# Eight experts of a mixture layer: the 128-column weight block as the stationary operand, loaded as two halves of 64 columns, with 96 token slots moving

## What is computed

```python
D_MODEL = 1024; SEQ = 256; N_EXPERTS = 8; TOP_K = 2; D_FF_EXPERT = 3584

def swiglu(h, w13, w2):
    gate, up = jnp.split(h @ w13, 2, axis=-1)
    return (jax.nn.silu(gate) * up) @ w2

def moe_swiglu(h, router, w13, w2):
    t = h.reshape(B * S, D)
    logits = (t @ router).astype(jnp.float32)
    top_val, top_idx = lax.top_k(logits, TOP_K)
    gate = jax.nn.softmax(top_val, axis=-1)
    combine = jnp.einsum('tk,tke->te', gate, jax.nn.one_hot(top_idx, N_EXPERTS, dtype=jnp.float32))
    out = jnp.zeros_like(t)
    for e in range(N_EXPERTS):
        out = out + combine[:, e:e + 1].astype(t.dtype) * swiglu(t, w13[e], w2[e])
```

## Time and profile before

| | |
|---|---|
| median of three runs | 2245.45 us (2242.42 to 2260.5) |
| the profiled execution's own time | 2243.6 us |
| its span, first to last instruction | 2241.8 us |
| granted TensorE clock, mean over the span | 0.983 |
| TensorE busy | 2155.9 us |
| VectorE (DVE) busy | 760.2 us |
| ScalarE (ACT) busy | 265.0 us |
| read from HBM | 460.96 MB |

### The profile page before, as it was taken

One profiled execution on the slowest core, in us unless ns is written; L12 is line 12 of the kernel. 1 busy time (PEld: TensorE's weight loads), 2 busy tenths in 40 slices (PEclk: granted clock), 3 DMA queues, 4 the chain that ended last, 5 costly groups with the idle time before them and its releaser, 6 DMA issues.

```text
span 2241.8 us, 20009 instructions
## 1 busy us (share of the span) xinstructions
PE 2155.9 (96%) x7476; PEld 1191.3 (53%) x7476; DVE 760.2 (34%) x2080; ACT 265.0 (12%) x549; POOL 192.6 (9%) x318
## 2 busy tenths in 40 slices
PE   8999989999799999997999999999999999999998
PEld 4454456776455788984444444444444444444443
DVE  2131231000343556533333343333423434324322
ACT  2121130000012333521000000000000000000000
POOL 1111101000103344220000000000000000000000
PEclk9999999999899899998999999999999999999999
DMA  9433425445410110027799999999899999999991
GB/s 348 150 113 113 150 75 187 150 150 165 150 32 2 22 24 17 13 81 226 258 313 307 314 307 317 315 303 328 301 316 316 309 323 307 310 315 308 353 310 63
DMA packets 353298, 474.14 MB, mean 212 GB/s; under 512 B 30105, under 2 KB 288433, under 8 KB 353217
## 3 DMA queue, kind: packets, MB, share of 16 engines
q1 hardware_dynamic: 349856, 460.96, 61.3%
q0 software_dynamic: 2336, 8.42, 1.1%
q10 hardware_dynamic: 1024, 3.67, 0.4%
HBM read 460.96 MB, written 12.06 MB: 211 GB/s over the span
## 4 chain that ended last, share of the span: by engine, by line
PE 91%; DVE 5%; ACT 2%; issue 1%; DMA 1%; POOL 1%; SPq 0%; DVEq 0%; POOLq 0%
PE ps L682 48%; PE ps L1258 17%; PE ps L796 11%; PE ps L734 7%; PE ps L747 2%; PE ps L850 1%; PE ps L957 1%; PE ps L763 1%; DVE arena L1842 1%; PE ps L1190 1%; DVE arena L1844 1%; PE ps L1197 0%; PE ps L781 0%; DMA arena<-wqkv 0%; ACT arena L1413 0%
## 5 line engine op out<-in xcount | busy, mean ns | idle before, releaser
L682 PE MATMUL ps<-arena 128*128 128x512 f32 (+10 forms) x4290 | 1159.9, 438 | 37.9 <-DVE arena L1829 8.3
L682 PEld LDWEIGHTS ps<-arena 128*128 128x128 f32 (+3 forms) x4290 | 638.3, 191 | 548.6 <-issue 488.4
L1258 PE MATMUL ps<-arena 128*128 128x512 f32 x896 | 392.5, 592 | 0.0
L2054 DVE STREAM_TRANSPOSE arena<-arena 32x128 f32<-32x128 f32 x1120 | 338.4, 302 | 19.0
L1258 PEld LDWEIGHTS ps<-arena 128*128 128x128 f32 x896 | 170.2, 190 | 213.8 <-issue 212.4
L2078 DVE TENSOR_TENSOR arena<-arena,ps 128x256 f32<-128x256 f32 x112 | 47.1, 421 | 658.3 <-ACT arena L1544 658.3
L796 PE MATMUL ps<-arena 128*128 128x512 f32 x576 | 253.5, 596 | 1.5 <-DMA arena<-wqkv 1.5
L796 PEld LDWEIGHTS ps<-arena 128*128 128x128 f32 x576 | 108.2, 192 | 128.3 <-issue 125.9
L1544 ACT ACTIVATE arena<-ps 128x256 f32<-128x256 f32 x112 | 43.1, 385 | 1005.2 <-PE ps L682 1005.2
L734 PE MATMUL ps<-arena 128*128 128x256 f32 x704 | 154.0, 381 | 0.0
L734 PEld LDWEIGHTS ps<-arena 128*128 128x128 f32 x704 | 134.7, 191 | 20.2 <-issue 1.9
(11 more groups left out here) (235 smaller groups left out, 912.9 us busy)
## 6 DMA issues: line engine op xcount, KB each, us to landing
arena<-mw SPq DMA_DIRECT2D x336, 1024.0 KB, 6.9
arena<-wqkv SPq DMA_DIRECT2D x36, 1024.0 KB, 7.8
arena<-fw SPq DMA_DIRECT2D x32, 1024.0 KB, 6.8
arena<-wrkv SPq DMA_DIRECT2D x12, 1024.0 KB, 7.3
arena<-awo SPq DMA_DIRECT2D x4, 1024.0 KB, 6.3
xg<-arena POOLq DMA_DIRECT2D x8, 512.0 KB, 10.1
arena<-bwo SPq DMA_DIRECT2D x4, 1024.0 KB, 10.1
arena<-xg SPq DMA_DIRECT2D x7, 512.0 KB, 7.7
```

What stands on the lines that cost most here:

```text
L682: last = mm(o, a, b, start=(n == 0), stop=(n == len(pairs) - 1))
L1258: last = mm(ps[:, 5 + h, :], hidT[:, g % 2, k, :], w[:, k, h * 512:(h + 1) * 512], start=(g == 0 and k == 0), stop=(g == GE // 2 - 1 and k ...
L2054: last = dve.transpose(dst[j * 32:(j + 1) * 32, :, i * 32:(i + 1) * 32], blocks[i * 32:(i + 1) * 32, :, j, :])
```

## The change

`CAP` is the number of slots of an expert, 96 instead of 128, for the gathered rows (`xg`), the results (`yd`) and every operand; an overflow pass still has 128. `OVER` is 5.

In an up unit each 128 x 128 block of the weights is now the stationary operand, in two halves of 64 columns (`COLS`), and the 96 token slots move. `by_halves` alternates the two halves, whose results go to PSUM partitions 0 to 63 and 64 to 127: 4 column blocks x 8 blocks of the contraction x 2 halves = 64 matmuls of 96 columns. A down unit likewise has 8 x 4 x 2 = 64. Results come out by feature, so that DVE's product is written straight into `hidT` and the turning of the products goes. What an expert gives is by feature too: ACT copies both banks to `yT`, DVE turns it with 24 transposes (`result_rows`), and for the last expert and overflow passes TensorE does it with 8 transposes. `next_picked` has 24 transposes, not 32, and moves from units 8 and 10 to 9 and 11. The overflow list has two entries an expert and is worked out after `shares`, right ahead of the loop. The weights that are read, their order, the ring and the DMAs of 1024 KB are the same.

```diff
-OVER = 3
+CAP = 96
+OVER = 5
...
+            COLS = (slice(0, RH), slice(RH, P))
+
+            def by_halves(o, pairs):
+
+                for n, (a, b) in enumerate(pairs):
+                    for c in COLS:
+                        last = mm(o[c], a[:, c], b, start=(n == 0), stop=(n == len(pairs) - 1))
                 return last
...
-                        run(ps[:, g % 4, :], [(picked[:, b, k, :], w[:, k, :]) for k in range(KB)]).then_inc(up_ps, 1)
+                        for f in range(4):
+                            last = by_halves(ps[:, g % 4, f * width:(f + 1) * width],
+                                             [(w[:, k, f * P:(f + 1) * P], picked[:, b, k, 0:width]) for k in range(KB)])
+                        last.then_inc(up_ps, 1)
                     else:
                         w = unit(u).rearrange("p (k n) -> p k n", n=D)
-                        pe.wait_ge(hidT_sb, n * (GE // 2) + (g + 1))
+                        pe.wait_ge(hide_sb, n * GE + (2 * g + 2))
                         if g == 0:
-                            pe.wait_ge(y_sb, n * 2 + 2)
-                        for h in range(2):
+                            pe.wait_ge(yT_sb, n * 2 + 2)
+                        for o in range(KB):
                             for k in range(4):
-                                last = mm(ps[:, 5 + h, :], hidT[:, g % 2, k, :], w[:, k, h * 512:(h + 1) * 512],
-                                          start=(g == 0 and k == 0), stop=(g == GE // 2 - 1 and k == 3), skip_group_check=True)
+                                for c in COLS:
+                                    last = mm(ps[c, 5 + o // 4, o % 4 * width:(o % 4 + 1) * width], w[:, k, o * P + c.start:o * P + c.stop],
+                                              hidT[:, g % 2, k, 0:width], start=(g == 0 and k == 0 and o % 4 == 0),
+                                              stop=(g == GE // 2 - 1 and k == 3), skip_group_check=True)
...
-            scatter(EXPERTS - 1, 1, 1)
+            result_rows(EXPERTS - 1, CAP)
+            scatter(EXPERTS - 1, 1, 1, CAP)
...
-                    dve.tensor_tensor(hid_e[:, pair % 2, g % 2, :], sg_e[:, g % 2, :], ps[:, g % 4, 256:512], ALU.mult).then_inc(hide_sb, 1)
-                    if g % 2:
-                        dve.wait_ge(hide_sb, n * GE + (g + 1))
-                        if pair >= 2:
-                            dve.wait_ge(down_ps, n * (GE // 2) + (pair - 1))
-                        turned(hidT[:, pair % 2], hid_e[:, pair % 2].rearrange("p a b -> p (a b)")).then_inc(hidT_sb, 1)
+                    if g % 2 == 0 and pair >= 2:
+                        dve.wait_ge(down_ps, n * (GE // 2) + (pair - 1))
+                    dve.tensor_tensor(hidT[:, pair % 2, g % 2 * 2:g % 2 * 2 + 2, 0:width], sg_e[:, g % 2, 0:2 * width].rearrange("p (f n) -> p f n", f=2),
+                                      ps[:, g % 4, 2 * width:4 * width].rearrange("p (f n) -> p f n", f=2), ALU.mult).then_inc(hide_sb, 1)
...
+            def result_rows(n):
+
+                for half in range(2):
+                    dve.wait_ge(yT_sb, n * 2 + (half + 3))
+                    if half == 0:
+                        dve.wait_ge(yd_out, n * 16 + 16)
+                    rows = yb[:, 512 * half:512 * half + 512].rearrange("p (k j f) -> p k j f", j=4, f=32)
+                    for i in range(CAP // 32):
+                        for j in range(4):
+                            last = dve.transpose(rows[i * 32:(i + 1) * 32, :, j, :], yT[j * 32:(j + 1) * 32, 4 * half:4 * half + 4, i * 32:(i + 1) * 32])
+                    last.then_inc(y_sb, 1)
```

More of the change, by code:

```diff
@@ L214, in build @@
         chosen = m.take(T, EXPERTS)
-        comb = m.take(T, EXPERTS + 1)
+        comb = m.take(T, 2 * EXPERTS + 1)
         place = m.take(T, EXPERTS + 1)
-        place2 = m.take(T, EXPERTS)
+        place2 = m.take(T, 2 * EXPERTS)
         cmp_a = m.take(T, EXPERTS, EXPERTS)
@@ L226, in build @@
         picked = m.take(2, KB, P)
-        hid_e = m.take(2, 2, 256)
+        yT = m.take(KB, P)
         sg_e = m.take(2, 256)
@@ L1217, in pick_transposes, with gather_half @@
                 last.then_inc(pickT_ps, 1)
-            def gather_half(b, half, back=None):
+            def gather_half(b, half, width, back=None):
                 if half and back is not None:
@@ L1223, in gather_half, with scatter @@
                     f = (4 * half + k) * P
-                    last = run(ps[:, (7, 4)[half], k * P:(k + 1) * P], [(xn[:, t, f:f + P], pick[:, b, t, :]) for t in range(T)])
+                    last = run(ps[:, (7, 4)[half], k * P:k * P + width], [(xn[:, t, f:f + P], pick[:, b, t, 0:width]) for t in range(T)])
                 last.then_inc(picked_ps, 1)
-            def scatter(n, b, back):
+            def scatter(n, b, back, width):
                 pe.wait_ge(y_sb, n * 2 + 4)
@@ L1260, in expert, with result_rows @@
                         last.then_inc(down_ps, 1)
+            def result_rows(n, width):
+                for half in range(2):
+                    pe.wait_ge(yT_sb, n * 2 + (half + 3))
+                    for k in range(4):
+                        last = pe.transpose(ps[0:width, half, k * P:(k + 1) * P], yT[:, 4 * half + k, 0:width], ident)
+                    last.then_inc(yrow_ps, 1)
             pe.wait_ge(pick_ok, 2)
-            gather_half(0, 0)
-            gather_half(0, 1)
+            gather_half(0, 0, CAP)
@@ L1286, in _ @@
                     pick_transposes(n + 1, 0, j + 3)
[L1287 to L1290, removed]
+                    gather_half(0, 0, P)
+                    gather_half(0, 1, P, j + 2)
+                    expert(n, n + 1, 0, over_plan, landed, P)
+                    result_rows(n, P)
+                    scatter(n, 0, j + 2, P)
         @block.scalar
```

155 lines of the change are left out of this document (89 added, 66 removed).

## The result

The change makes the kernel faster: 2163.17 us (2158.15 to 2173.14, four runs) against 2245.08, a ratio of 0.963 with the interval 0.958 to 0.968. Forecast were 2246 us and no change. The profiled execution took 2160.95 us, its span is 2159.1.

The account below looks back on a forecast made before the run. The prediction took TensorE's matmul time to bound the kernel, and one DMA engine delayed by instruction packets after the change: 2243.6 - 1154.1 + 1154.5 + 1.5 = 2245.5, said as 2246 us; eight in ten, 2045 to 2430.

Parts of the forecast that it names:

- TensorE's pace: Expert matmuls: the two halves run side by side, 64 records a side at 82.5 ns, 5.28 us a unit for 6.87.
- The number of packets: TensorE's instruction fetch: the larger loop body does not stay on the engine, so about 170 packets of 16 KB come.
- The DMA's own pace: Weight loads in the stage: 122.7 us an expert, 5.84 a unit, above TensorE's 5.28, so the DMA sets the pace.
- the packets' term: Expert stage: 21.3 instruction packets an expert at 1.2 us each, added to the DMA's 122.7 us, give 148.3.
- The step that failed, first: DMA in the stage: each instruction packet sets one engine back 1.1 to 1.6 us, 1.2 taken; that engine bounds, 7.06 a unit.
- The step that failed, second: TensorE's instruction packets in the stage: each was charged only to the DMA, 1.11 us of one engine.
- both signs that I had named for my case: In the stage TensorE's idle time ends with "DMA arena<-mw", and units are 7.1 us apart with single engines trailing.
- Case A: DMA in the stage: packets don't line up on one engine or cost less, 5.91 us a unit, 2060 us; chance 0.36.
- my two cases: Expert stage: packets bound one DMA engine, 2246 us, chance 0.38; or they spread or cost less, 2060 us, chance 0.36.
- Q: TensorE's sequencer becomes the bound in the stage: 2396 us at 30 ns an instruction, 2650 at 36; chance 0.22.
- N: TensorE in the stage: the clock falls or a half waits for the other, 10.6 us a unit; chance 0.04.
- S': DMA in the stage: one engine is the bound and a packet costs it 1.57 us, 2306 us in all; chance 0.11.

Follow-up runs that it names:

- e7: The changed kernel with half of the contraction left out of each expert unit's matmuls, all weights still loaded: 2068.68 us, one run.
- e4: The changed kernel with half the bytes of each expert unit loaded and TensorE's instructions the same: 1997.97 us, one run.
- e1: The changed kernel with every fourth 128x128 block of a unit loaded whole, the others in halves: 2144.21 us, ratio 0.956.
- e6: The kernel of e5 with TensorE's loop over experts 0 to 5 written out: 2094.31 us, ratio 0.932.
- e5: The kernel of e1 with whole blocks moved together, last in even units, first in odd, side by side in down units: 2113.72 us, ratio 0.942.
- e11: The changed kernel with a whole block only in two units of four, in the order of e5: 2116.33 us, one run.
- e8: The changed kernel with nothing but TensorE's loop written out: 2176.65 us.
- e10: The kernel of e8 timed once more, beside the changed kernel: 2177.11 us, ratio 0.973.
- e2: The changed kernel with all blocks loaded whole, 128 columns at a time, no halves: 2298.42 us, one run.
- e3: The changed kernel with only the first 32 of the 96 slots moving in the expert matmuls: 2248.78 us, one run.

## Why the prediction was wrong

**What held.** TensorE's pace: 128 records in 5.28 us between the gaps, the halves side by side. The number of packets (172 for 170), and that the loop's body does not stay. The DMA's own pace without the packets' term, 5.84 forecast and 5.91 in e7. DVE's work hidden, 249 us less of it for 220. Ahead of the stage `choose` began 2.6 us earlier, at 1063.16, as worked out, and the stage 3.1 earlier. Behind it the scatter began 2.5 us after the last down unit for 0.8, +1.7 for +2.4 forecast; the timeline's last DVE row answers to that of the earlier trace rows:

```profile
2152.91 0.07 DVE L2217 MEMSET arena<- 128x11 f32 x1 [2.93 <-issue]
```

Five untaken turns have 2.93 us of "issue" for 2.60 with three, not the 4.3 that I had by proportion: part of that was a fixed time. Outside the stage the two profiled executions took 1089.5 and 1088.9 us; +1.5 was forecast.

**The step that failed, first.** "So a packet sets one engine back by 1.1 us (its own time) to 1.6", and, if all go to the same engine, "that engine is the bound". It was 25.6 us an expert in the sum, 1.2 us a unit. e7 shows the ring running at 361 GB/s with a packet every second unit, where this step gives 331; the changed kernel's 6.38 us a unit is under the 7.06 that it gives, too. I had read it from one tail that may have been the ordinary unevenness at the end of a transfer. No row shows which engines the packets use, those of the kernel before included, which the sum put on one; whether they use different ones, or one engine makes it good, stays open.

**The step that failed, second.** I counted what a page costs the DMA and never what it costs TensorE: "1.11 us of one engine, not spread over sixteen" is the only term, and TensorE's wait for a page was put at nothing without a reason. A page now lasts 5.2 us in place of the 50 it lasted before, and the round trip of 6.3 us doesn't fit into that. The runs show this term at 185 us of the stage, nearly all of it in the 154 counted gaps. So the idle time ended with "issue" and not with "DMA arena<-mw", and the ring was full, against both signs that I had named for my case. Case A (2060) had the DMA right and lacked these, too; the measured time lies between my two cases for a reason that neither had. The trace of before could have warned: the earlier trace rows has two packets in 9.5 us, 9.3 apart, the densest in its straight code, so that nothing showed pages coming at 5.3. The Trainium skill ("Runtime: NRT & Kernel Launch", section "Instruction fetch mechanics") calls the cost of a block's boundary (a block is what I call an instruction page) mostly hidden. The trace after disagrees with 1.2 us at nearly each; e4 agrees, where the DMA is loaded with half the bytes.

**The rivals.** Q, the sequencer: four instructions every 82 ns, 21 ns each over whole pages, so issue is not the bound. The Trainium skill's 62 ns for each matmul, which it gives for decoding by software ("TensorE: Matmul & The Clock Gate", section "Wait — 56ns, not 53.3ns?"), are not what this trace has: a matmul comes every 41 ns. N: the clock stayed at 0.99 over the stage, in spite of the stalls; in e7 it did fall, to 0.84, where TensorE waits for the ring. S', the packet at 1.57 us, falls with the first step.

**The sum as it should have been.** A unit lasts the longest of three: TensorE's work (5.28), the DMA (5.84 to 5.91), and its pages by their round trip (1.01 x 6.3 = 6.4). Measured 6.38.

## What to carry to other kernels

Count the instructions of an edit as well as its work: in these runs a page of 256 TensorE instructions had to last longer than the time in which the next one came in (6.3 us beside a DMA at 341 GB/s, under 5.3 at 208), or the page stalled the engine, in the trace as "issue" gaps at equal numbers of records, not at the borders of the work. Where it is close, fewer and longer instructions in part of the work can beat the form that is fastest by itself (e1 to e6: 2163 to 2094 us with slower matmuls), if the two kinds change places seldom and yet no page is left with short instructions alone (e5, e11). And look at who waits for a ring slot before naming the DMA as the bound: the DMA share was 0.98 over the stage, and yet SyncE waited 805 us for TensorE.

## What the runs showed of the hardware that was not expected

- A page's packet starts 3.8 us after TensorE resumes, takes 1.09 and lets TensorE go on 1.41 us after it has landed, while the DMA moves 341 GB/s; at 208 GB/s (e4) the packet starts after 1.9. With straight code in place of a loop the first is 4.0 to 4.2 us from the second third of the stage on (e8, e10).
- A jump back over 42 units of code stalls TensorE 5.1 and 5.5 us (3.3 to 5.5 in e1 and e5, 2.9 to 3.1 in e2, 3.9 to 4.1 in e4).
- Going from matmuls in 64-column halves to one of 128 columns costs 0.14 us over the pace, back 0.17.
- With whole blocks of 128 columns as weights and 96 columns moving a record comes every 112 ns (e2); two halves of 64 take 82 ns for the same block.
- With 32 columns moving in place of 96, TensorE never idle, the granted clock is 0.50 (1.2 GHz) from 1114 us to the end of the stage (e3); with 96 and a stall of 1.2 us in every 6.3 it is 0.99.
